# Sharing expert rows between TensorE and VectorE in both fronts, and splitting steps of VectorE and GpSimd from their products

## The reference

```
for each layer, for prompt and sample:
    h  = modulate(rms_norm(x), ...)                    # gates and shifts come from w_mod
    z  = h @ w_in                                      # A, B, C: queries, keys, values; D: pooling and latent
                                                       # queries; E: latent keys and rotary key
    o  = neighbourhood attention | pooling | latent attention
    x += g1 * (o @ w_out)
    h2 = modulate(rms_norm(x), ...)
    q  = h2 @ peer_wq ; scores against sub-keys ; top 16 of each of 8 heads -> expert e, gate g
    x += g2 * sum over 8 x 16 experts of  g * gelu(h2 . peer_u[e]) * peer_v[e]
```

## Time and profile before

| | |
|---|---|
| time, median of 3 runs | 4238.35 us (4236.18 to 4253.35) |
| profiled execution | 4231.16 us, its span 4229.4 us |
| TensorE busy | 3607.1 us, 85% of the span |
| VectorE busy | 2564.7 us, 61% |
| GpSimd busy | 2582.1 us, 61% |
| ScalarE busy | 959.1 us, 23% |
| expert gathers (queue 0) | 82.2% of 16 DMA engines' span |
| HBM read | 1511.70 MB, 359 GB/s |

### The profile page before, as it was taken

How to read it: one execution, slowest core, us unless ns; L and a number is a source line. 1 busy time by engine, 2 the same in 40 slices (tenths; PEclk the granted TensorE clock), 3 DMA queues, 4 the chain that set the end, 5 groups by cost and what they waited for, 6 DMA issues and landing times.

```text
span 4229.4 us, 37631 instructions
## 1 busy us (share of the span) xinstructions
PE 3607.1 (85%) x10514; PEld 1679.1 (40%) x10514; DVE 2564.7 (61%) x6453; ACT 959.1 (23%) x2479; POOL 2582.1 (61%) x2833
## 2 busy tenths in 40 slices
PE   7889899989978888888887899999898887777776
PEld 2355444545434223443342355554443432222222
DVE  1175557767655446566666555677676666666664
ACT  1212222223221112222222222232232122221211
POOL 0057446666665556676667663566676677777776
PEclk9899999999999999999999999999999999999999
DMA  6477899999999999999999988999999999999999
GB/s 241 161 266 273 296 337 388 362 389 405 358 367 379 385 390 349 344 356 360 393 401 408 353 290 297 366 367 392 392 407 351 369 402 409 407 405 405 399 403 356
DMA packets 472260, 1519.96 MB, mean 359 GB/s; under 512 B 59980, under 2 KB 78704, under 8 KB 471544
## 3 DMA queue, kind: packets, MB, share of 16 engines
q0 software_dynamic: 368640, 1342.34, 82.2%
q1 hardware_dynamic: 103416, 175.21, 11.6%
HBM read 1511.70 MB, written 5.67 MB: 359 GB/s over the span
## 4 chain that ended last, share of the span: by engine, by line
PE 41%; DMA 27%; POOL 15%; issue 9%; DVE 5%; ACT 2%; SPq 1%; DVEq 0%; POOLq 0%; ACTq 0%
DMA expert_rows<-in_peer_v,experts 22%; PE expert_sum L2112 21%; POOL expert_rows L1033 14%; DMA expert_rows<-in_peer_u,experts 4%; PE work L1871 4%; PE work L1845 3%; PE work L2063 3%; PE work L2078 2%; PE work L2007 2%; PE work L2034 2%; PE work L1819 2%; DVE expert_rows L1779 2%; POOL stat_rstd L983 1%; PE work L2052 1%; PE work L1963 1%
## 5 line engine op out<-in xcount | busy, mean ns | idle before, releaser
L2112 PE MATMUL expert_sum<-expert_rows,weight_diagonals 128*128 128x512 f32 x5080 | 2464.5, 615 | 450.6 <-DMA expert_rows<-in_peer_v,experts 419.8
L1779 DVE CUSTOM_DVE_ANT_0 expert_rows<-expert_rows,tokens 128x1024 f32<-128x1024 f32 x1280 | 1557.0, 1217 | 837.7 <-DMA expert_rows<-in_peer_u,experts 834.0
L1033 POOL DMA_INDIRECT expert_rows<-in_peer_v,experts x1280 | 1231.1, 962 | 915.2 <-PE expert_sum L2112 703.3
L2112 PEld LDWEIGHTS expert_sum<-expert_rows,weight_diagonals 128*128 128x128 f32 x5080 | 904.6, 193 | 1674.7 <-issue 1363.3
L1033 POOL DMA_INDIRECT expert_rows<-in_peer_u,experts x1280 | 1216.6, 950 | 452.8 <-issue 348.5
L1315 ACT ACTIVATE weight_diagonals<-ident,expert_weights 128x128 f32<-128x128 f32 x1270 | 447.2, 392 | 585.5 <-PE expert_sum L2112 355.3
L1871 PE MATMUL work<-weight_ring,h_or_mixed 128*128 128x384 f32 (+3 forms) x800 | 246.6, 462 | 4.1 <-DMA weight_ring<-in_w_in 2.3
L1819 PE MATMUL work<-ident,scratch 128*128 128x128 f32 (+1 forms) x782 | 130.6, 290 | 99.4 <-DVE scratch L1411 36.4
L1845 PE MATMUL work<-weight_ring,silu_cond 128*2 128x512 f32 x384 | 176.1, 613 | 12.0 <-DMA weight_ring<-in_w_mod 11.1
L1871 PEld LDWEIGHTS work<-weight_ring,h_or_mixed 128*128 128x128 f32 x800 | 143.9, 191 | 106.8 <-issue 49.5
L1819 PEld LDWEIGHTS work<-ident,scratch 128*128 128x128 f32 (+1 forms) x782 | 99.4, 146 | 195.3 <-issue 73.5
(11 more groups left out here) (176 smaller groups left out, 2481.2 us busy)
## 6 DMA issues: line engine op xcount, KB each, us to landing
weight_ring<-in_w_mod SPq DMA_DIRECT2D x24, 2048.0 KB, 11.0
weight_ring<-in_w_out SPq DMA_DIRECT2D x16, 2048.0 KB, 19.4
weight_ring<-in_peer_wq SPq DMA_DIRECT2D x16, 2048.0 KB, 10.0
expert_rows<-in_peer_u,experts POOLq DMA_INDIRECT x1280, 7.3
expert_rows<-in_peer_v,experts POOLq DMA_INDIRECT x1280, 7.3
weight_ring<-in_w_in SPq DMA_DIRECT2D x12, 1536.0 KB, 9.5
weight_ring<-in_w_in SPq DMA_DIRECT2D x4, 2048.0 KB, 15.2
weight_ring<-in_t_pool SPq DMA_DIRECT2D x4, 2048.0 KB, 10.7
```

Source lines behind the costliest of these rows:

```text
L1033: g.indirect_dma_start(buffer, None, table, bass.IndirectOffsetOnAxis(ap=idx_st[:, col:col + 1], axis=0),).then_inc(row_in, 16)
L1779: v_.tensor_tensor_reduce(out=u_ring[r % U_RING], in0=u_ring[r % U_RING], in1=tokens[:, :], scale=1.0, scalar=0.0, op0=ALU.mult, op1=ALU.a ...
L2112: ins = t_.matmul(acc[:, hf * 512:(hf + 1) * 512], diags[:, at * P:(at + 1) * P], v_buffer(row)[:, hf * 512:(hf + 1) * 512], start=first = ...
```

## The change

Odd rows go to VectorE in three stretches in place of one: rows 0 to 75, rows 642 to 717 and the last 20. A row is added 20 steps behind its number, so these are the steps 20 to 95 and 662 to 737. The steps "hs" (head sums and roots) and "oe" (adding the output product to x) are new in the list. "hs" holds what VectorE and GpSimd did at "pr", "up" and "kv", with a cost of 0; "oe" holds what VectorE did at "o", and each of the two now costs 4.4. In mixer_out the wait for the product moves behind the copy of the gates. Everything that referred to the update of x at "o" refers to "oe", the banks of "o" among them.

```
-SHARED_ROWS = ((ALL_ROWS - 20, ALL_ROWS),)
+SHARED_ROWS = ((0, 76), (642, 718), (ALL_ROWS - 20, ALL_ROWS))
...
-            "kT": 1.3, "py": 0.4, "pp": 3.5, "s": 1.0, "pt": 1.0, "pv": 0.6, "ot": 1.8, "o": 8.8}.get(kind, 0.2)
+            "kT": 1.3, "py": 0.4, "pp": 3.5, "s": 1.0, "pt": 1.0, "pv": 0.6, "ot": 1.8, "o": 4.4, "oe": 4.4,
+            "hs": 0.0}.get(kind, 0.2)
...
-                  + [("pr", *k) for k in products[i:i + 1]]]
+                  + [s for k in products[i:i + 1] for s in (("pr", *k), ("hs", *k))]]
...
-        out += [("pr", "D", l, b) for b in blocks[i:i + 1]]
+        out += [s for b in blocks[i:i + 1] for s in (("pr", "D", l, b), ("hs", "D", l, b))]
...
-        out += [("up", l, b) for b in blocks[i - 1:i] if i]
+        out += [s for b in blocks[i - 1:i] if i for s in (("up", l, b), ("hs", "uq", l, b))]
...
-        out += [("kv", l, b) for b in keys[j - 1:j] if j >= 1]
+        out += [s for b in keys[j - 1:j] if j >= 1 for s in (("kv", l, b), ("hs", "ukv", l, b))]
...
-            out += [("o", l, blocks[i], 0), ("o", l, blocks[i], 1)]
+            out += [s for j in range(2) for s in (("o", l, blocks[i], j), ("oe", l, blocks[i], j))]
...
-        return [(("g", 0, l, b, j), 1, step), (step, 1, step)]
+        return [(("g", 0, l, b, j), 1, ("oe", l, b, j)), (step, 1, ("oe", l, b, j))]
...
-            def project(ch, l, b):
-                if ch != "C":
-                    n, mul, add = {"A": (HEADS, 1.0, DH * EPS), "B": (HEADS, 1.0 / DH, EPS),
-                                   "D": (1, 1.0 / QR, EPS), "E": (1, 1.0 / KVR, EPS)}[ch]
-                    rstd((ch, l, b), n, mul, add)
...
+            def head_roots(k, l, b):
+                n, mul, add = {"A": (HEADS, 1.0, DH * EPS), "B": (HEADS, 1.0 / DH, EPS), "D": (1, 1.0 / QR, EPS),
+                               "E": (1, 1.0 / KVR, EPS), "uq": (HEADS, 1.0, QK * EPS),
+                               "ukv": (HEADS, 1.0 / QK, EPS)}[k]
+                rstd((k, l, b), n, mul, add)
...
-            def project(ch, l, b):
-
-                key = (ch, l, b)
-                if ch in "AB":
+            def sums_of_heads(k, l, b):
+
+                key = (k, l, b)
+                if k in ("A", "B"):
                     head_sums(key, heads(sq[:, 0:WIDTH]))
-                elif ch == "D" and not pooled_later(l, b):
+                elif k in ("uq", "ukv"):
+                    head_sums(key, heads(sq))
+                elif k == "D" and not pooled_later(l, b):
...
                 dve.wait_ge(*banks.filled(gkey))
-                dve.wait_ge(*banks.filled(step))
                 v_.tensor_copy(gated, bank(gkey)).then_inc(banks.frees(gkey), 1)
                 dve.wait_ge(*banks.freed(gkey))
+                dve.wait_ge(*banks.filled(step))
                 v_.tensor_tensor(gated, bank(step), gated, ALU.mult).then_inc(banks.frees(step), 1)
```

More of the change, by code:

```diff
@@ L231, in heads_of_prompt @@
     b = 0
[L232 to L236, removed]
+    return [("pr", "A", l, b), ("hs", "A", l, b), ("pr", "B", l, b), ("hs", "B", l, b), ("sc", "A", l, b),
+            ("pr", "C", l, b), ("tu", "A", l, b), ("sc", "B", l, b), ("pr", "D", l, b), ("hs", "D", l, b),
+            ("tu", "B", l, b), ("sc", "D", l, b), ("pr", "E", l, b), ("hs", "E", l, b), ("cq", l, b),
+            ("sc", "E", l, b), ("up", l, b), ("hs", "uq", l, b), ("ck", l, b), ("us", l, b), ("kp", l, b),
+            ("uT", l, b), ("kv", l, b), ("hs", "ukv", l, b), ("pd", l, 0, 0), ("py", l, 0, b), ("ks", l, b),
+            ("pd", l, 0, 1), ("py", l, 1, b), ("kT", l, b)]
 def heads_of(l, blocks):
@@ L258, in heads_of @@
         out += ends.pop(0) if ends else []
-        out += [("pr", "D", l, b) for b in blocks[i:i + 1]]
+        out += [s for b in blocks[i:i + 1] for s in (("pr", "D", l, b), ("hs", "D", l, b))]
         out += later[j:j + 1] if j >= 0 else []
-        out += [("pr", "E", l, b) for b in blocks[j:j + 1] if j >= 0]
-        out += [("up", l, b) for b in blocks[i - 1:i] if i]
+        out += [s for b in blocks[j:j + 1] if j >= 0 for s in (("pr", "E", l, b), ("hs", "E", l, b))]
+        out += [s for b in blocks[i - 1:i] if i for s in (("up", l, b), ("hs", "uq", l, b))]
         out += [("kp", l, b) for b in keys[j - 1:j] if j >= 1]
@@ L636, in build @@
             kind = step[0]
-            if kind == "nx" or kind == "pr" and step[1] != "C":
+            if kind in ("nx", "hs"):
                 stat_turns += [step[1:]]
+            if kind == "pr" and step[1] != "C":
+                sq_turns += [step[1:]]
             elif kind in ("up", "kv"):
-                stat_turns += [("uq" if kind == "up" else "ukv", *step[1:])]
-            if kind == "pr" and step[1] != "C" or kind in ("up", "kv"):
-                sq_turns += [stat_turns[-1]]
+                sq_turns += [("uq" if kind == "up" else "ukv", *step[1:])]
             if kind == "sc":
@@ L728, in build @@
         rope_step = sem("rope_step")
-        pool_in_ready = Steps(sem("pool_in_ready"), [s[2:] if s[0] == "pr" else s[1:] for s in of_kind("pr", "pp")
+        pool_in_ready = Steps(sem("pool_in_ready"), [s[2:] if s[0] == "hs" else s[1:] for s in of_kind("hs", "pp")
                                                              if s[0] == "pp" or s[1] == "D" and not pooled_later(*s[2:])])
-        rope_keys = Steps(sem("rope_keys_copied"), [s[2:] for s in of_kind("pr") if s[1] == "E"])
+        rope_keys = Steps(sem("rope_keys_copied"), [s[2:] for s in of_kind("hs") if s[1] == "E"])
         values_ready = Steps(sem("mla_values_ready"), [s[1:] for s in of_kind("kp")])
@@ L868, in load_gate_bias @@
                 if l:
-                    sp.wait_ge(*x_updated.done(("fin", NB - 1) if which else ("o", 0, NB - 1, 1)))
+                    sp.wait_ge(*x_updated.done(("fin", NB - 1) if which else ("oe", 0, NB - 1, 1)))
                 at = (3 * which + 2) * D
@@ L1057, in expert_row @@
                     row_u(r + U_RING)
-            does = {"nx": norm, "pr": project, "up": queries_up, "kv": keys_up, "us": rope_queries,
+            does = {"nx": norm, "hs": head_roots, "us": rope_queries,
                     "ks": rope_keys_of, "row": expert_row}
@@ L1083, in norm @@
                 if k == "n2":
-                    sc.wait_ge(*x_updated.done(("o", l, b, 1)))
+                    sc.wait_ge(*x_updated.done(("oe", l, b, 1)))
                     if b == 0:
@@ L1604, in mixer_out @@
                     dve.wait_ge(xs_in, 48 * (l + 1))
-                if prior(of_o, step):
-                    dve.wait_ge(*x_updated.done(prior(of_o, step)))
+                if prior(of_oe, ("oe", l, b, j)):
+                    dve.wait_ge(*x_updated.done(prior(of_oe, ("oe", l, b, j))))
                 dve.wait_ge(*banks.filled(gkey))
-                dve.wait_ge(*banks.filled(step))
                 v_.tensor_copy(gated, bank(gkey)).then_inc(banks.frees(gkey), 1)
                 dve.wait_ge(*banks.freed(gkey))
+                dve.wait_ge(*banks.filled(step))
                 v_.tensor_tensor(gated, bank(step), gated, ALU.mult).then_inc(banks.frees(step), 1)
```

19 lines of the change are left out of this document (6 added, 13 removed).

## The result

The changed kernel took 4252.6 us (median of 15 runs, 4244.7 to 4262.1) where the kernel before took 4237.1 us: a ratio of 1.0038, 95% interval 1.0028 to 1.0047. That is 16 us slower, where 70 us of gain had been forecast, and lies above the range.

The account below looks back on a forecast made before the run. Gathers of expert rows were taken to set the pace outside the two fronts, TensorE inside them. From the 4238 us median, -102.7 + 27.5 + 12 - 7 = -70 us gave 4168 us, range 4115 to 4222 us.

Parts of the forecast that it names:

- The bound: TensorE sets the pace in the two fronts (287 to 612, 2372 to 2700 us), gathers of expert rows outside them.
- the price of an addition: VectorE's additions in the fronts, 1.28 us each, were to cost TensorE's path nothing beyond the 5% overlap loss.
- The relief: Both fronts: 76 row sums off TensorE, 102.7 us less with perfect overlap, 27.5 us added back for imperfect overlap.
- the sign by which I wanted to know the order: In the profile after: TensorE idle before transposes, waiting for VectorE's scaling or GpSimd's roots, would show the order at fault.
- The three terms of a stretch: Each front stretch lasts as long as the largest of TensorE, DMA and GpSimd time; sums 276.6 of 325, 273.7 of 328 us.
- My own table: Stretch 345:450 us of the first front: TensorE 83.5, DMA 81.6, GpSimd 88.6 us, the largest.
- The order of the roots: 23 head sums and roots in the fronts move behind the next row, 0 to 2.5 us each, 0.5 taken: 12 us lost.
- The split output step: At 14 products outside the fronts, gates early and output later: 0 to 1.2 us each, 0.5 taken, 7 us gained.
- The gain stays: Behind the fronts the gathers run at their own pace whenever they start, so time gained in the fronts is kept.
- The order eats it: Rival, chance 0.12: all 23 moved roots on TensorE's path at 2.5 us, 57 us, leaving 13 us gain, 4225 us.
- the likeliest case: The forecast as summed, chance 0.66: 4168 us, its own range 4130 to 4205 us.
- the slower case with VectorE: Rival, chance 0.09: 76 additions delay what TensorE waits for, 242 us against 131 freed, 111 us slower, 4349 us.

Follow-up runs that it names:

- the filler: Kernel before with odd rows of both fronts shared, plus two TensorE matmuls with zeros in place of each lost row sum: ratio 1.0084, 37 us slower.
- sharing alone: Kernel before with only the odd rows of both fronts given to VectorE; sums, roots and output steps unmoved: ratio 0.9979, 9 us faster.
- the moved steps alone: Kernel before with only the "hs" edits, head sums and roots behind the product; no rows shared in the fronts: ratio 1.0053, 24 us slower.
- the runs without rotation: Kernel before without GpSimd's rotation of latent queries and keys: ratio 0.9980; the same with odd rows of both fronts shared: 0.9971.
- only the root moved: Kernel of the moved steps alone, with VectorE's sums and copies back at the product; GpSimd's roots stay moved: ratio 1.0062, 27 us slower than before.
- half the filler: As the filler, but only the first of the two zero matmuls per lost row sum: ratio 1.0020 against the kernel before, 9 us slower.

## Why the prediction was wrong

**The bound** was read right as far as it went: TensorE held up the gathers in the fronts, and taking its relief back costs up to 46 us, so it was on the path. But I took a busy share of nine tenths for a bound of nine tenths. The fronts are a chain over four engines, and less work on one of them shortens it only where that one isn't waiting next.

**The step that failed first is the price of an addition**, "I take nothing beyond the 5%, as every step has VectorE idle time ahead of TensorE's products". It measured up to 0.5 us an addition, 37 us in all. The 149 us of idle time were there, but a static order puts the addition where it stands in the list and not where VectorE is idle: in the heads it stands ahead of sums and scalings that TensorE's transposes wait for. The row stretches put half of it there: with the filler, 9 us more in row steps 35 to 59 and 9 in 675 to 695; the other half is spread over the rest of the fronts.

**The relief, -102.7 + 27.5 = -75 us, was mis-sized**: 46 us at most. By the windows above, sharing took 76 row sums of 1.72 us, 131 us, off TensorE, but its busy time fell by only 90 us (610.1 to 519.9), as the matmuls that stayed got longer. Of these 90 us, 84 came back as idle time, and the fronts got 6.7 us shorter. TensorE's idle time ahead of its transposes, 29.2 and 21.0 us before, is 53.8 and 49.9 with sharing alone and 30.2 and 25.4 with the moved steps alone: the sign by which I wanted to know the order came mostly from the sharing. The three terms of a stretch (TensorE, DMA, GpSimd) treat waits between engines as if they shrank with the longest. In the heads they didn't. The chain of work there shows it, shares by line, first before (row steps 35 to 59 of the first trace):

```profile
by line: POOL expert_rows L1033 23.3%; issue 14.6%; PE expert_sum L2112 10.6%; PE work L1871 9.0%; POOL stat_rstd L983 7.5%; DVE expert_rows L1779 5.8%; PE work L1904 3.7%; DVE scratch L1447 3.6%; DVE scratch L1455 3.0%; POOL scratch L1014 
```

and then in the kernel with sharing alone:

```profile
by line: POOL expert_rows L1033 36.7%; issue 23.7%; POOL stat_rstd L983 9.4%; POOL scratch L1014 6.4%; POOL scratch L1019 4.1%; POOL scratch L1021 4.0%; DVE scratch L1455 3.5%; DVE scratch L1447 3.4%; PE expert_sum L2112 2.2%; POOL stat_bia
```

The row sum fell from 10.6 to 2.2% of the chain and the projection's line (L1871) is no longer among the largest; GpSimd's lines and the issue gaps are over four fifths of it. How the chain divides is not firm for one kernel, though. In the second trace of the kernel before the same row steps took the same time, and TensorE had more of it:

```profile
by line: PE work L1871 18.8%; PE expert_sum L2112 18.6%; issue 17.0%; POOL expert_rows L1033 7.2%; DVE expert_rows L1779 5.8%; PE work L1941 4.1%; PE work L1819 4.1%; PE work L1904 3.7%; POOL stat_rstd L983 3.7%; DVE scratch L1447 2.2%; DVE
```

In both, sharing moves the chain from TensorE to GpSimd. My own table had said that GpSimd comes next: 88.6 us against TensorE's 83.5. The row steps took 112 us, since the pieces on GpSimd don't stand back to back: it was busy 77.5 us, and its idle time ended above all with VectorE (11.6 us) and in issue gaps (11.2 us). That GpSimd's amount alone isn't it, the runs without rotation show.

**The order of the roots**, "between 0 and 2.5 us each, I take 0.5", was mis-sized by half: 24 us in all for the moved steps, 27 with only the root moved. The row stretches of the run with moved steps put 10.4 us in row steps 0 to 20, where seven of the 23 steps are, 6.7 in 21 to 95 with nine, and 9.5 in 663 to 737 with seven, that is 1.2 us for each. Row steps 0 to 20 are the surest: 66.6 us with the moved steps, 67.1 with only the root moved and 67.1 in the changed kernel, against 55.8 to 57.3 in all traces without. The 15 moved between row steps 408 and 591 cost nothing that can be seen (587.5 us, before 588.8), since the gathers set the pace there. The slack of "a later product and a row in between" isn't there for D: its scaling is wanted by the very next transposes, as in the timeline.

**The clock** is a cost that the prediction didn't have. It fell from 0.98 and 0.96 to 0.88 and 0.85 in the fronts, and to 0.89 and 0.87 with sharing alone. The 41 us between the 131 us taken off TensorE and the 90 us by which its busy time fell are an estimate of what it cost in busy time. Its share of the loss in time isn't settled: over whole fronts half the filler took back 18 of 46 us, near the even 23, while row steps 703 to 720 were 4.5 us shorter with it, in single executions.

**The split output step**, 7 us, measured 4 us with an interval of 5 either way: right in size, and too small to tell. **"The gain stays"** isn't settled. Row steps 96 to 219 took 10.5 us longer in the changed kernel than before, and 397.0 us with sharing alone against 391.5; the traces of the experiments without sharing or with few shared rows lie between 391.5 and 398.0 there.

**Two sums on record don't come out as stated.** "The order eats it" takes 57 us from the 70, but the 70 already held 12 of them: 25 us would be left, 4213 us, not 13 and 4225. And the range of the likeliest case, with losses of 0 to 10% and both order terms at either end, is 4118 to 4248 us and not 4130 to 4205. By its own terms the forecast reached past the kernel before, and 4253 us still lies outside.

Of the rivals, the order eating the gain and the slower case with VectorE both happened in part: 24 and 37 us against 46, and 4 for the output step, make 11 us slower of the 16 measured. VectorE didn't become a bound, it was busy 224 of 331 us; the additions cost by their place in the order. I had treated as alternatives what adds.

## What to carry to other kernels

An engine that is busy nine tenths isn't a bound whose work can be subtracted; take the chain of waits through one period, remove the piece, and see what waits for whom next. An engine with half its time idle isn't free either: in a static order a new instruction can cost up to its full length wherever something that others wait for stands behind it, so give such work only to steps where the chain waits for another engine for long (here the output product: 18 additions there brought as much as 76 everywhere). A short step that heads a chain, like a root, must not be moved behind gathers that are long and wait for buffers themselves, where TensorE sets the pace; where the gathers set it, the same move cost nothing here. And a filler that takes a relief back should be checked against the busy time of the engine that it fills.

## What the runs showed of the hardware

- Relief can lower TensorE's clock so far that its busy time doesn't fall: with 35 matmuls fewer in a stretch it was busy 80.9 us instead of 81.8, at a granted clock of 0.83 instead of 0.99, and 16 matmuls with zeros brought the clock to 0.93. Other traces without sharing were busy 81.5 to 86.7 us there, at 0.94 to 0.99. A row sum took 3.62 us at a granted clock of 0.50, behind a wait of 5.70 us, and 1.88 us at 1.00, behind a wait of 1.54 us.
- A VectorE instruction with two SBUF inputs lengthens GpSimd's gathers: 1008 ns each with them in the first front, 971 ns when one input came from PSUM, 974 ns in the kernel before. Of the gathers in the two fronts that started while an addition ran, the 22 with two SBUF inputs took 1.44 us in the median and up to 2.02, the 23 with one took 0.95 and at most 1.05. Of the 37 us that sharing costs with the filler, some 8 are this by the two medians, with overlapping intervals.
- Every fourth row on VectorE was slower than every second (1.0020 and 0.9979), and lost it in the heads of the first front. Unexplained.
